# Handing over between phases with two tokens past a group and eight gathers in flight

## The reference

```python
act = jax.nn.gelu(jnp.einsum('thkd,td->thk', u_tab[expert], xb))
return jnp.einsum('thk,thkd->td', gate * act, v_tab[expert])
```

## Time and profile before

| | us |
|---|---|
| median of 3 runs | 4410.25 |
| lowest and highest | 4400.0, 4410.38 |
| profiled execution, its own time | 4404.23 |
| its span, first to last instruction | 4402.1 |

### The profile page before, as it was taken

One profiled execution on the slowest core, in us unless ns is written; L12 is line 12 of the kernel. 1 busy time (PEld: TensorE's weight loads), 2 busy tenths in 40 slices (PEclk: granted clock), 3 DMA queues, 4 the chain that ended last, 5 costly groups with the idle time before them and its releaser, 6 DMA issues. The chain is left out here.

```text
span 4402.1 us, 46784 instructions
## 1 busy us (share of the span) xinstructions
PE 3206.2 (73%) x15781; PEld 1734.2 (39%) x15781; DVE 2480.9 (56%) x7734; ACT 804.7 (18%) x1299; POOL 1645.8 (37%) x1380
## 2 busy tenths in 40 slices
PE   5999997775597776766688666677665666677676
PEld 2998896754164542431155333144111111111111
DVE  2435554138764546777665554677775555555555
ACT  4223323342123112210014111211000010000000
POOL 2111104524255543543255444354333333333332
PEclk8999998977798986977789888698666666666666
DMA  8011003424799989989899999999899999999998
GB/s 339 26 60 60 31 30 129 127 98 145 292 373 370 364 354 359 378 346 364 322 383 410 360 358 361 384 412 364 356 399 361 412 415 404 411 415 404 415 413 345
DMA packets 225975, 1359.01 MB, mean 309 GB/s; under 512 B 29286, under 2 KB 38406, under 8 KB 83532
## 3 DMA queue, kind: packets, MB, share of 16 engines
q0 software_dynamic: 156672, 1140.92, 64.3%
q1 hardware_dynamic: 69068, 215.09, 13.4%
HBM read 1322.56 MB, written 33.35 MB: 308 GB/s over the span
## 5 line engine op out<-in xcount | busy, mean ns | idle before, releaser
L1083 DVE CUSTOM_DVE_ANT_0 peer_uv<-peer_uv,all_PS 128x512 f32<-128x512 f32 x2176 | 1435.4, 685 | 1140.3 <-PE all_PS L1021 585.5
L1021 PE MATMUL all_PS<-peer_hT,peer_sel 96*128 96x512 bf16 x2176 | 972.8, 463 | 949.3 <-DVE peer_halves L1083 799.0
L1004 POOL DMA_INDIRECT peer_uv<-in_uv,peer_idx x1088 | 1041.5, 957 | 1600.3 <-PE all_PS L1041 1198.8
L1021 PEld LDWEIGHTS all_PS<-peer_hT,peer_sel 96*128 96x128 bf16 x2176 | 205.0, 101 | 1776.3 <-DVE peer_halves L1083 1291.7
L1041 PE MATMUL all_PS<-peer_uv,peer_zw 128*32 128x512 f32 x4352 | 835.0, 869 | 1.5 <-DVE peer_zw L1103 1.5
L888 POOL TENSOR_TENSOR flow_w_lo<-flow_w,flow_w_hi 128x1024 fp32r<-128x1024 f32 (+1 forms) x204 | 460.4, 2262 | 541.1 <-ACT flow_w_hi L881 537.3
L1057 ACT ACTIVATE peer_ge<-peer_pre 128x4 f32<-128x4 f32 x272 | 56.1, 206 | 2121.4 <-DVE peer_pre L1089 1955.9
L1041 PEld LDWEIGHTS all_PS<-peer_uv,peer_zw 128*32 128x32 f32 x4352 | 154.0, 142 | 423.8 <-issue 422.0
L908 PE MATMUL all_PS<-mix_h_hi,flow_w_hi 128*128 128x384 f32 (+1 forms) x672 | 281.7, 419 | 31.6 <-POOL flow_w_lo L888 31.6
L881 ACT ACTIVATE flow_w_hi<-flow_w 128x1024 fp32r<-128x1024 f32 (+1 forms) x204 | 203.6, 1004 | 327.3 <-PE all_PS L910 134.9
L910 PE MATMUL all_PS<-mix_h_hi,flow_w_lo 128*128 128x384 f32 (+1 forms) x672 | 224.6, 334 | 0.0
(11 more groups left out here) (294 smaller groups left out, 4679.6 us busy)
## 6 DMA issues: line engine op xcount, KB each, us to landing
cond_w<-in_w_ada SPq DMA_DIRECT2D x12, 2048.0 KB, 11.8
flow_w<-in_w_gate_ab SPq DMA_DIRECT2D x48, 512.0 KB
flow_w<-in_w_query SPq DMA_DIRECT2D x48, 512.0 KB
flow_w<-in_w_conv SPq DMA_DIRECT2D x36, 512.0 KB
peer_uv<-in_uv,peer_idx POOLq DMA_INDIRECT x1088
gla_w<-in_w_heads SPq DMA_DIRECT2D x24, 512.0 KB, 3.9
flow_w<-in_w_proj_b SPq DMA_DIRECT2D x24, 512.0 KB
flow_w<-in_w_out SPq DMA_DIRECT2D x24, 512.0 KB
```

Source lines behind the costliest of these rows:

```text
L1004: self.nc.gpsimd.indirect_dma_start(out=self.uv[:, n % self.NUV, :], out_offset=None, in_=self.A["uv"], in_offset=bass.IndirectOffsetOnAxi ...
L1021: nc.tensor.matmul(PS[:, f, :], self.sel[:, c:c + 1].broadcast_to([3 * GR, P]), self.hT[:, g % self.NH, f * 512:(f + 1) * 512], start=True ...
L1083: nc.vector.tensor_tensor_reduce(part, part, PS[:, f, :], 1.0, 0.0, ALU.mult, ALU.add, self.halves[:, d, f, e:e + 1]).then_inc(M["dotted"], 1)
```

## The change

`Gather.fetch` gets a flag `full`: with it GpSimd fetches `FULL` = 10 - 2 = 8 tokens past the mark instead of 4. Each phase from mix to pick calls it once more at its end with the mark `hi`; norm, pick (which has nothing else on GpSimd) now have that one call alone. The marks are moved so that each is a multiple of 4 plus 2: part 0 ends at 26, part 1 has 90, 126, 154, 182, 246, 318, part 2 402, 450, 486, 522, 606, 702. At such a mark PE has just summed a group, so that all eight gathers have a slot. The waits in `fetch` are the same, and so is all arithmetic.

```diff
--- before.py
+++ after.py
@@ -953,6 +953,7 @@
 
 
     NUV, NZ, ND, NH, AHEAD = 10, 3, 4, 5, 4
+    FULL = NUV - 2
     NIDX = 6
 
     def __init__(self, nc, A, G, sc):
@@ -992,9 +993,10 @@
         self.at[engine] = max(first, upto)
         return range(first, upto)
 
-    def fetch(self, pool, upto):
-
-        for n in self.steps("pool", upto + self.AHEAD if upto else 0):
+    def fetch(self, pool, upto, full=False):
+
+        assert not full or upto in (0, T) or upto % BT == 2
+        for n in self.steps("pool", upto + (self.FULL if full else self.AHEAD) if upto else 0):
             u, c, j = self.tokens[n]
             if n == self.before[u]:
                 pool.wait_ge(self.M["idx_set"], u + 1)
@@ -1191,6 +1193,7 @@
             for j in range(NJ):
                 gat.fetch(pool, turns.upto(j))
                 w.make_low(nc, pool, w0 + j + w.pairs)
+            gat.fetch(pool, hi, True)
 
         @block.tensor
         def _(pe):
@@ -1439,9 +1444,7 @@
 
         @block.gpsimd
         def _(pool):
-            gat.fetch(pool, turns.before())
-            for j in range(NJ):
-                gat.fetch(pool, turns.upto(j))
+            gat.fetch(pool, hi, True)
 
         @block.tensor
         def _(pe):
@@ -1735,9 +1739,7 @@
 
         @block.gpsimd
         def _(pool):
-            for j in range(NJ):
-                if j >= early:
-                    gat.fetch(pool, upto(j))
+            gat.fetch(pool, hi, True)
 
         @block.tensor
         def _(pe):
@@ -2006,10 +2008,10 @@
                 w0, lo, done = 0, 0, 0
                 for part in PARTS:
                     if part.index == 0:
-                        marks = [0, 0, 0, 0, 0, 0, 24]
+                        marks = [0, 0, 0, 0, 0, 0, 26]
                     else:
-                        span = gat.before[part.tiles[0]] - lo
-                        marks = [lo + span * sum(SHARES[:i]) // sum(SHARES) for i in range(len(SHARES) + 1)]
+                        span = gat.before[part.tiles[0]] - 2 - lo
+                        marks = [lo + span * sum(SHARES[:i]) // sum(SHARES) // BT * BT for i in range(len(SHARES) + 1)]
                     part.m_before = done
                     done += 4 * len(part.tiles)
                     with Scope(nc, f"mid{part.index}") as mid:
```

## The result

The change made the kernel slower: 4544.85 us (median of 4 runs, 4537.16 to 4551.5) against 4407.39 us (4 runs, 4400.0 to 4410.38), a ratio of 1.031 with a 95% interval of 1.029 to 1.034. That is +137 us where the prediction said +95; it lies within the range given (4442 to 4548), near its upper end. The profiled execution took 4546.79 us, its span is 4545.0 against 4402.1 before.

A forecast was written before the change was run, and what follows sets the result against it. From mix1 on, DMA's gather traffic plus its standing at 13 hand-overs was taken as the bound; start terms 32 + 22 + 18 + 10 + 13 gave +95 us, a median of 4503 us, range 4442 to 4548.

The forecast's parts named there:

- item 2: At the 13 phase starts: no gathers follow the restart until a group is free, so DMA stands longer, +95 us in all.
- item 5: Moved marks: two tokens per part cross each border, a product more or less beside a token, DMA's work the same: nothing.
- keys1, keys2: Starts of the keys phases: restart like pick, but with 2 MB of loads and a weight's low half ahead, +5 us each.
- the 10 to 20 of the forecast: Expected sign: a phase's first gather comes 10 to 20 us after the DRAIN.
- The 1.5 us to the first bytes: At each restart: assumed delay of about 1.5 us until a free group's first gather moves bytes.
- Item 3: Phase ends: issuing the last four gathers takes GpSimd 5 us, hidden while the DRAIN awaits landing; otherwise 65 us.
- Item 4: norm and pick in one fetch: order of gathers the same up to the four at the end, so nothing.
- The upper one: Upper bound: PE and DVE cannot use eight landed tokens, so all 13 hand-overs lose 10.4 us: 135 us, 4545.
- the third rival: Engines bound mix and merge: nothing caught up there and low clock costs more, +135 and over, 4545; chance 0.15.
- The first (the number in flight does not matter to the DRAIN): Hand-overs: DRAIN as long as today for another reason; -10 us, 4394, or 4400 as median; chance 0.08.
- the second (quick catching up, +39): After restarts: landed tokens used fast, only the removed start overlap remains, some 3 us per boundary, about 4449; chance 0.13.
- the signs: Expected trace marks: DRAIN median, DMA share after last landing, first gather's delay, last phase's 2.6 us a gather, ACT's o copy.

The follow-up runs named there:

- e1_full4: The change with four instead of eight gathers in flight at a phase's end, new marks and single fetch kept: 4426.7 us, +27 against the kernel before.
- e5_full4_round: e1_full4 with the step boundaries of pick1 and pick2 rounded up by a third: 4408.9 us, +8 against the kernel before.
- e2_after_nodrain: The change with blocks that close without GpSimd's DRAIN: 4428.9 us, +29 against the kernel before.
- e8_end0: The change with no gather past the mark at a phase's end: 4450.6 us, +49 against the kernel before.
- e12_mid_drain: e8_end0 with one more GpSimd DRAIN in the middle of mix1 and mix2: 4461.7 us, +56 against the kernel before.

## Why the prediction was right, and where it was off

*The mechanism* (GpSimd's DRAIN at the block's end waits for gathers in flight, the engines for it) held. It had been read from coincidence in time; taking the DRAIN away gives 108 of the change's 137 us back, and 48 us in the kernel before. One part of it was not seen: the time from the last landing to the DRAIN's end, which I took by the kind of phase (1.6, 3.4, 4), goes by the number of gathers since the last such DRAIN.

*The number* was too low by 42 us: 16 of them are DMA's longer standing at the starts (item 2), the rest its standing elsewhere, most of it in pick1 (item 5). The total lies 3 us inside the range, whose upper end stood for the flight alone; that the unforeseen part of the marks still fitted under it is luck. A slip beside it: 95 us on the median of 4410 are 4505, not 4503.

*Item 2, the sum by starts.* I compare it with DMA's standing time in both profiled executions, added up from its packets from a phase's last dot to 30 us behind the restart.

| starts | forecast, us | measured, us |
|---|---|---|
| last, pick1, pick2 | +22 | +24 |
| keys1, keys2 | +10 | +18 |
| out1, out2 | +22 | +20 |
| norm1, norm2 | +18 | +22 |
| merge1, merge2 | +10 | +11 |
| mix1, mix2 | +13 | +16 |
| together | +95 | +111 |

Kind by kind the terms are near. keys is the one mis-sized: the first gather there comes 10.0 and 10.3 us after the DRAIN, but in keys1 only one follows at once (+11.6); the third comes at +21.0 us, behind a low half (2.4 us) and another operation of GpSimd (L1608, 2.1 us) and what these wait for, where I gave 3 us. In keys2 four come at once, the fifth at +21.9. In mix the first gather comes 22 to 25 us after the DRAIN, past the 10 to 20 of the forecast. The 1.5 us to the first bytes, which no row had shown, was well taken: in 11 of the change's 13 starts the first packet moves 1.6 us after the first gather's record begins, in the other two after 1.9 and 2.5.

*Item 5, "marks: nothing"*, is the step that failed. It counted products beside tokens and DMA's bytes, and not where PE's sum falls between DVE's steps. Outside these stretches DMA stands 28 us more (from 1080 us on, added up from its packets), 22 of it in pick1. By e1_full4 against before the marks cost 27 us, and 19 of them went with e5_full4_round's other boundaries. The clue stood in the earlier trace rows: half of DVE's idle time before the dots (585.5 of 1140.3 us) is ended by PE's spread.

*Item 3*, issuing is hidden while the DRAIN waits for landing and costs 65 us otherwise, was shown in its second half by e2_after_nodrain (53 us). *Item 4*, the single fetch, costs little or nothing: e5_full4_round, which has it, is 8 us from before, with an interval from nothing to 12.

*The bounds.* The upper one, 135 us for losing all of 10.4 us at each of 13, was met by the total (137), but with 110 to 122 from the flight and the rest from the marks. So four more in flight cost 8.5 to 9.4 of a possible 10.4 us: the engines made little use of the eight tokens ready at a restart. That is the third rival's number, 4545, and its mechanism held as far as nothing is caught up in mix1 (3.17 us a token in both); but it named mix and merge alone, and out1 (2.91 in both) and keys1 (3.21 and 3.20) catch up as little. Whether the low clock after longer standing costs something beside it, as the rival has it, was not separated.

*Rivals.* The first (the number in flight does not matter to the DRAIN) is out by the series of four, six, eight; the second (quick catching up, +39) by the time and by the unchanged pace. Of the signs, the DRAINs' median was 18.5 us against about 20 and none was under 15; DMA's share in the 40 us behind the last landing was 0.48 to 0.68 in eleven starts and 0.74 and 0.80 in keys, against 0.5 to 0.7. The last phase kept its 2.6 to 2.7 us a gather, and ACT took the last piece of o at 1423.4, 7.8 us after merge1's start, as forecast:

```profile
1423.38 0.84 ACT L942 ACTIVATE merge_o_hi<-merge_o_in 128x768 fp32r<-128x768 f32 x1 [0.84 <-DMA merge_o_in<-scratch_ob]
```

*Open.* Of the 77 us between the two kernels without the DRAIN 53 are the issuing and about 19 the alignment (e1_full4 against e5_full4_round); with a mark at 2 mod 4 PE's own DRAIN takes 3.1 us at the end of pick2, since it ends with a sum, and no run separates that. Nor was it tried whether clearing the semaphores on another engine would let eight gathers be issued across the barrier.

## What to carry to other kernels

Work issued ahead of a barrier bridges it only if nothing at the barrier waits for that work, or for its issue: look at which engine's DRAIN ends last, compare it with the last landing and with the last instruction before it, and do not read the DRAIN's length as its price. Before cutting deeper into a prefetch, try whether the block needs that engine's DRAIN at all. And when a mark or a step count is shifted by two, count again which of one engine's steps lie beside which of another's.

## What the runs showed of the hardware

- GpSimd's DRAIN at a block's end has work of its own for every indirect gather issued since the last such DRAIN, landed or not. With 84, 64, 34 and 25 gathers behind it, and all landed, it took 9.32, 7.69, 5.23 and 4.50 us (e8_end0, e12_mid_drain): 0.082 us a gather over 2.4, of which the last low half makes 2.34. Where gathers were in flight, the DRAIN ended 1.5 us after the last packet behind 28 gathers (at norm1 of the change), 3.1 behind 64 (pick1) and 4.4 behind 96 (the last phase), 0.043 us a gather; part of the work seems to go on beside the transfers, which no run shows by itself. Over the kernel before's 13 hand-overs these tails make 38 us.
- The Trainium skill (Perfetto Trace Analysis, Sequencer-only Instruction (DRAIN, etc)) has the recorded interval of such an instruction begin when its semaphores are satisfied and end when it has executed. The 7 us of e8_end0 in which nothing else was at work fit that, as executing. But the record also holds what is no work of the DRAIN's own: in e8_end0 the 2.34 us of the low half before it, and in the change the landing of gathers, up to 3503.7 in a record that began at 3487.0.
- GpSimd's DRAINs are of two kinds. In e2_after_nodrain the one at line 110 took 4.6 us with four gathers to be issued, and the next ones at lines 110 and 111 at most 0.05 right behind that, with the four just issued still moving. The one at line 108 waits for landing, as above.
